# Hybrid attention/retention trunk on one core: upper near keys multiplied only with the queries behind them, their probability blocks transposed with 64 rows

## What is computed

```python
ATTN_GROUPS = ((128, 1), (512, 4), (2048, 16))      # window, dilation

def dilated_window_attention(q, k, v, window, dilation):
    # query t attends keys t - j*dilation, j = 0..window//dilation
    ...
    scores = einsum(q, k) * (dh ** -0.5)
    scores = where(mask, scores, -inf)              # causal, band of the window
    m = scores.max(-1); pr = exp(scores - m); denom = pr.sum(-1)
    out = einsum(pr, v) / denom
    lse = m + log(denom)
...
weights = softmax(stack(lses, 0), axis=0)           # over the three groups
attn = (weights * stack(outs, 0)).sum(0)
```

## Time and profile before

| what | value |
|---|---|
| median of three runs | 1498.9 us (1498.19 to 1499.43) |
| the profiled execution | 1498.79 us |
| its span, first to last instruction | 1497.0 us |
| mean granted TensorE clock | 0.999 |
| TensorE busy | 1483.8 us, 99% |
| weight loads busy | 1317.8 us, 88% |
| VectorE busy | 997.5 us, 67% |
| ScalarE busy | 787.6 us, 53% |
| DMA, mean | 178 GB/s |

### The profile page before, as it was taken

How to read it: one execution, slowest core, us unless ns; L and a number is a source line. 1 busy time by engine, 2 the same in 40 slices (tenths; PEclk the granted TensorE clock), 3 DMA queues, 4 the chain that set the end, 5 groups by cost and what they waited for, 6 DMA issues and landing times.

```text
span 1497.0 us, 20942 instructions
## 1 busy us (share of the span) xinstructions
PE 1483.8 (99%) x8716; PEld 1317.8 (88%) x8716; DVE 997.5 (67%) x1118; ACT 787.6 (53%) x834; POOL 45.1 (3%) x24
## 2 busy tenths in 40 slices
PE   9999999999999999999999999999999999999998
PEld 8898898988988988888888988989889888888886
DVE  6665665756655688777866656666566556887777
ACT  5364463644644456656534645546446444566562
POOL 0000000000000010000010000000000000100000
PEclk9999999999999999999999999999999999999999
DMA  9544546455556565656555554454445565655571
GB/s 294 196 155 158 167 141 197 146 164 169 169 169 212 170 220 172 206 191 220 169 169 169 169 169 147 163 175 163 160 150 173 176 215 170 211 199 193 172 237 40
DMA packets 231486, 265.83 MB, mean 178 GB/s; under 512 B 4208, under 2 KB 221808, under 8 KB 230768
## 3 DMA queue, kind: packets, MB, share of 16 engines
q1 hardware_dynamic: 231264, 264.57, 53.3%
q10 hardware_dynamic: 144, 0.13, 0.1%
HBM read 263.64 MB, written 1.05 MB: 177 GB/s over the span
## 4 chain that ended last, share of the span: by engine, by line
PE 93%; DVE 4%; DMA 1%; ACT 1%; issue 1%; SPq 0%; DVEq 0%; ACTq 0%
PE bank L1264 35%; PE bank L1269 18%; PE bank L1238 8%; PE bank L1240 8%; PE bank L1239 8%; PE acc L1238 3%; PE acc L1239 3%; PE acc L1240 3%; PE acc L1407 1%; PE acc L1382 1%; DVE w_lo L731 1%; PE acc L1362 1%; PE acc L1405 1%; PE acc L1378 1%; DMA raw<-w_in 1%
## 5 line engine op out<-in xcount | busy, mean ns | idle before, releaser
L731 DVE TENSOR_TENSOR w_lo<-raw,w_hi 128x2048 fp32r<-128x2048 f32 x239 | 547.3, 2290 | 273.0 <-ACT w_hi L395 272.7
L395 ACT ACTIVATE w_hi<-raw 128x2048 fp32r<-128x2048 f32 x242 | 461.6, 1908 | 146.6 <-PE bank L1240 81.4
L1264 PE MATMUL bank<-xT_both,w_hi 128*128 128x512 f32 x1952 | 466.3, 391 | 0.6 <-DVE mid_lo L955 0.6
L1264 PEld LDWEIGHTS bank<-xT_both,w_hi 128*128 128x128 f32 x1952 | 359.8, 188 | 71.6 <-issue 1.2
L1269 PEld LDWEIGHTS bank<-xT_both,w_lo 128*128 128x128 f32 x1952 | 250.3, 191 | 9.5
L1269 PE MATMUL bank<-xT_both,w_lo 128*128 128x256 f32 x1952 | 253.2, 283 | 0.0
L1238 PE MATMUL bank<-w_hi,xT_both 128*128 128x256 f32 (+1 forms) x528 | 176.9, 335 | 3.4 <-DVE w_lo L731 1.7
L1240 PE MATMUL bank<-w_hi,xT_both 128*128 128x256 f32 (+1 forms) x528 | 175.6, 333 | 0.0
L1239 PE MATMUL bank<-w_lo,xT_both 128*128 128x256 f32 (+1 forms) x528 | 175.6, 332 | 0.0
L494 ACT ACTIVATE scratch<-bank 128x512 f32<-128x512 f32 x64 | 38.2, 597 | 220.1 <-PE bank L1269 220.1
L1238 PEld LDWEIGHTS bank<-w_hi,xT_both 128*128 128x128 f32 x528 | 101.0, 191 | 14.8 <-issue 4.7
(11 more groups left out here) (167 smaller groups left out, 1611.0 us busy)
## 6 DMA issues: line engine op xcount, KB each, us to landing
raw<-w_in SPq DMA_DIRECT2D x134, 1024.0 KB, 5.0
raw<-w_up SPq DMA_DIRECT2D x44, 1024.0 KB, 5.1
raw<-w_down SPq DMA_DIRECT2D x20, 1024.0 KB, 5.0
raw<-w_ret_proj SPq DMA_DIRECT2D x16, 1024.0 KB, 5.0
raw<-w_attn_proj SPq DMA_DIRECT2D x8, 1024.0 KB, 5.0
raw<-w_out SPq DMA_DIRECT2D x8, 1024.0 KB, 5.0
raw<-w_ple_gate SPq DMA_DIRECT2D x8, 1024.0 KB, 5.0
scratch<-ln_rows SPq DMA_DIRECT2D x4, 1024.0 KB, 7.8
```

The source lines that it names most:

```text
L395: nc.scalar.activation(w_hi[:, s, :], raw[:, s, :], ACT.Copy).then_inc(hi_ready, 1)
L731: nc.vector.tensor_tensor(w_lo[:, s, :], raw[:, s, :], w_hi[:, s, :].bitcast(F32), ALU.subtract).then_inc(lo_ready, 1)
L1264: mm(pair[p][:, m, :], hi[:, o:o + P], src[:, k0 + k, :, :].rearrange("p a t -> p (a t)"), start=first and k == 0, stop=False)
```

## The change

Two edits, both on TensorE; no wait, semaphore, buffer or DMA is changed, and the instructions of the other engines are the same.

```diff
@@ transpose_prob
-                        ins = nc.tensor.transpose(acc[t][:, o * P:(o + 1) * P], prob[:, t, o * P:(o + 1) * P], ident)
+                        q = slice(P // TT if o == 1 else 0, P)
+                        ins = nc.tensor.transpose(acc[t][:, o * P + q.start:(o + 1) * P], prob[q, t, o * P:(o + 1) * P],
+                                                  ident[q, q])
@@ attend
+                    by_query = acc[a][:, 0:SEQ].rearrange("p (t q) -> p t q", t=TT)
                     for t in range(TT):
-                        mm(acc[a][:, 0:SEQ].rearrange("p (t q) -> p t q", t=TT), att_v0[:, (done - 1) % 2, t, d],
-                           probT[:, a, :, t * P:(t + 1) * P], start=(t == 0), stop=False)
+                        q = slice(t * P // TT, P)
+                        mm(by_query[:, :, q], att_v0[:, (done - 1) % 2, t, d],
+                           probT[:, a, :, t * P + t * P // TT:(t + 1) * P], start=(t == 0), stop=False)
```

## The result

The changed kernel takes 1503.61 us (median of 7 runs, 1503.14 to 1504.62) against 1499.43 (7 runs, 1498.19 to 1500.06): 4.2 us or 0.32% slower, ratio 1.0032 with a 95% interval of 1.0023 to 1.0041. The forecast was 1504.4, worked out as 5.5 us over 1498.9.

A forecast was written before the change was run, and what follows sets the result against it. The prediction took TensorE's written order as the bound. Its terms, -3.3 (attend), -1.6 (smaller transposes) and +10.4 (changes of tile), gave +5.5 us on 1498.9: 1504.4 us, range 1493.8 to 1509.5.

The forecast's parts named there:

- pass-through of 1: On TensorE: time taken from or added to one of its instructions comes out at the end nearly one for one.
- Attend: In attend, 32 second-near-block matmuls go from 256 to 128 moving columns, 0.104 us less each: 3.3 us less.
- The small transposes' own gain: In the transposes' calls, 32 transposes of 64 columns each gain 0.049 us: 1.6 us less, bounds 0 and 1.7.
- The change of tile: Around the 64-row transposes, 64 changes of the array's tile cost 0.163 us each, emptying alone: 10.4 us more, bounds 0 and 15.5.
- case C: Rival at the tile changes: emptying and bare weight load in sequence, 0.24 us each; 1509.5 us; chance 0.17 including higher prices.
- the forecast's band of 0.12 to 0.2 us: The range of prices per change of tile counted as the forecast's own case, chance 0.27.
- Who waits behind it: ScalarE's copies behind transposes ending 0.55 us later a call: covered by a chunk of projection, so TensorE alone pays.
- A: Rival at the tile changes: no price, only the smaller columns count; 1494.0 us, 0.33% faster; chance 0.33.
- B: Rival at the tile changes: only the weight load is bare, 0.08 us each; 1499.1 us; chance 0.23 including nearby prices.
- D: Rival in attend: two runs of 64 columns cost as much as 256 columns, so 3.3 us are missing; no chance of its own.

The follow-up runs named there:

- The attend half alone: The changed kernel with all eight transposes of a call back at 128 rows and 128 columns, keeping attend's smaller matmuls: 1495.44 us, ratio 0.9975.
- the transposing half: The changed kernel with attend multiplying all 256 columns again, keeping the 64-row transposes: 1506.48 us, ratio 1.0052.
- the small ones last: The changed kernel with each call's six full transposes first and its two 64-row ones last, next to each other: 1500.13 us, ratio 1.0008.
- two small blocks: The changed kernel with 64-row transposes also for the last block of each tile, so 4 small ones a call: 1512.64 us, ratio 1.0091.

## Why the prediction was right

**What bounds the kernel.** TensorE's own order, with a pass-through of 1: borne out. The attend half alone gave 3.7 us (2.2 to 5.1 by its interval) for a sum of 3.3, and the transposing half 7.4 for 7.7 of longer calls in the trace.

**Attend, 3.3 us less.** Right: four matmuls in 0.66 us in place of 0.86, the two smaller ones in two runs of 64 columns at the price of their columns.

**The small transposes' own gain, 1.6 us.** It never shows by itself, since the changes cover it. Inside the small tile it is there: the second of two neighbours holds 0.15, of which 0.09 are the emptying, so 0.06 in place of 0.11. The step took 0.061.

**The change of tile, 0.163 us each, 10.4 in all.** This term was too large, and put together from the wrong parts. The longer calls give 7.7 us net; with the small transposes' 32 x 0.05 = 1.6 us added back that is 9.3, or 0.145 for each of the 64. The step took the whole of a transpose's length that lies under its successor (0.163) as emptying, and let the weight load go on meanwhile. The rows show the reverse on both: TensorE takes up the next load 0.20 us after the start of a transpose that lasts 0.27, so emptying adds 0.09, and the load is not done meanwhile: 0.05 of it is bare. The two errors nearly cancel (0.09 + 0.05 = 0.14). The price of case C, emptying and bare load one after the other, had the right mechanism, but with 0.163 for an emptying of 0.09, and with 0.08 for a bare load of 0.05, read from a projection matmul. So the size fell in the forecast's band of 0.12 to 0.2 us partly by luck. With 0.145 in place of 0.163 the prediction's own sum gives 9.3 - 4.9 = +4.4 us, and the medians differ by 4.2. The eight loads of a call run over 1.36 us, where it looked for 1.43.

**Who waits behind it.** Nearly as said. In the timeline of ScalarE, answering to the earlier trace rows:

```profile
89.31 0.58 ACT L505 ACTIVATE scratch<-bank 128x512 f32<-128x512 f32 x1
90.10 1.09 ACT L416 ACTIVATE scratch<-acc 128x512 f32<-128x512 f32 x2 [0.21 <-PE acc L1363]
92.29 0.53 ACT L464 ACTIVATE mid_hi<-scratch 128x384 fp32r<-128x384 f32 x1 [1.10 <-DVE scratch L922]
```

The copies now wait 0.21 us for the transposes, and ScalarE's idle time behind them shrinks from 1.43 to 1.10. TensorE waits for none of it. The 0.8 us by which its wait for `w_lo` has grown stand at 23 us, before the first transposes. The same wait is 0.69 us with the small ones last and 0.29 with two small blocks, and it is missing in the traces of both halves alone. So it differs between traces that have run the same TensorE order up to there; what sets it isn't shown.

**The rivals.** A (no price) would have been 1494.0. It is what the kernel becomes without its small transposes, but for their 1.6 us: 1495.4. B needed a price near 0.08, C one of 0.24, D needed attend to gain nothing; none of them holds. C's 1509.5 is 6 us above the measured time, though its mechanism is the one that the rows show.

## What to carry to other kernels

Where TensorE is the bound, count the places at which the size of the array's tile changes before halving the rows of a matmul: here each costs some 0.14 us, more than the whole 0.11 us of a full float32 transpose, and a 64-row transpose saves only 0.05. Fewer moving columns in the same tile gave their full value here, in attend. If small tiles can't be avoided, put them next to each other, and on different rows and in different PSUM banks where the data allow, since those ran side by side. Even then a call was 0.18 us longer than with eight full transposes: of all arrangements tried, leaving the transposes whole is the best.

## What had not been expected

A change of tile has two costs, and a small matmul between full ones pays both on each of its sides: 0.09 us of emptying behind the matmul before the change, whether this has 128 or 64 columns, and the bare weight load of the matmul behind the change, 0.05 us for a transpose and about 0.10 for a projection matmul. The idle time shows only on the weight loads (0.17 us, "issue") and never on the matmuls, whose modelled lengths overlap: TensorE reads as 99% busy in each of these kernels. And two transposes of 64 rows on different rows of the array, into different banks, start within 0.01 us of each other, their weight loads too.
